# Weight panels of two attentions' neighbours, moved into the attentions in pieces

## The reference, cut to what matters

```python
# first block: differential attention of six heads with two maps each, and attention to a memory
kv = rms_norm(mem, mem_norm_g) @ w_mem_kv          # once for block a, once for block b
proj = h @ w_in                                    # q, k, v, q_mem
a = softmax(q0 @ k0 + bias) - lam * softmax(q1 @ k1 + bias);  o = a @ v
om = softmax(q_mem @ k_mem * 64 ** -0.5) @ v_mem
x = x + concat(rms_norm(o), om) @ w_out
# second block, odd layer: 16 heads of 64, S = 256 is one block, so plain causal attention
q, k, v, g = split(x @ w_in_odd)
o = softmax(rope(q) @ rope(k) * 64 ** -0.5, causal) @ v
x = layer_norm(alpha * x + (o * silu(g)) @ w_out_odd)
```

## Time and profile before

| | |
|---|---|
| runs | 3120.51, 3126.64, 3128.22 us, median 3126.64 us |
| profiled execution, first to last instruction (span; the page gives no other time for it) | 3122.5 us |
| PE busy | 3014.5 us, 97% |
| DVE busy | 2007.9 us, 64% |
| ACT busy | 1512.8 us, 48% |
| mean granted TensorE clock | 0.989 |
| bytes moved | 606.10 MB, mean 194 GB/s |

### The profile page before, as it was taken

One profiled execution on the slowest core, in us unless ns is written; L12 is line 12 of the kernel. 1 busy time (PEld: TensorE's weight loads), 2 busy tenths in 40 slices (PEclk: granted clock), 3 DMA queues, 4 the chain that ended last, 5 costly groups with the idle time before them and its releaser, 6 DMA issues. The chain is left out here.

```text
span 3122.5 us, 43115 instructions
## 1 busy us (share of the span) xinstructions
PE 3014.5 (97%) x17959; PEld 2637.2 (84%) x17959; DVE 2007.9 (64%) x2237; ACT 1512.8 (48%) x1692; POOL 24.1 (1%) x41
## 2 busy tenths in 40 slices
PE   7999998899999999999999999999999999999998
PEld 6889897788888899778888888998789798997898
DVE  4547647555455467498898987554555756787755
ACT  4543343334344345477777776443434445432453
POOL 0001000000000000000000000000000000000000
PEclk9999999999999999999999999999999999999999
DMA  5338650065555567599999998541445143345142
GB/s 194 132 124 265 223 185 28 9 242 189 188 189 184 173 211 243 201 361 351 354 363 350 370 349 298 174 145 60 141 167 177 42 162 135 135 152 177 55 169 95
DMA packets 197852, 606.10 MB, mean 194 GB/s; under 512 B 19648, under 2 KB 59401, under 8 KB 154394
## 3 DMA queue, kind: packets, MB, share of 16 engines
q1 hardware_dynamic: 192306, 588.23, 53.0%
q0 software_dynamic: 3872, 12.71, 1.3%
q10 hardware_dynamic: 1480, 2.41, 0.3%
HBM read 602.26 MB, written 1.05 MB: 193 GB/s over the span
## 5 line engine op out<-in xcount | busy, mean ns | idle before, releaser
L2121 DVE TENSOR_TENSOR w_lo<-ring,w_hi 128x2048 fp32r<-128x2048 f32 x336 | 769.7, 2292 | 336.2 <-ACT w_hi L2016 331.0
L2016 ACT ACTIVATE w_hi<-ring 128x2048 fp32r<-128x2048 f32 x336 | 643.1, 1915 | 367.4 <-PE ps L1963 153.4
L358 DVE TENSOR_TENSOR w_lo<-ring,w_hi 128x2048 fp32r<-128x2048 f32 (+2 forms) x209 | 469.4, 2247 | 480.1 <-ACT w_hi L349 479.4
L349 ACT ACTIVATE w_hi<-ring 128x2048 fp32r<-128x2048 f32 (+2 forms) x209 | 392.7, 1881 | 645.1 <-PE ps L470 488.4
L470 PE MATMUL ps<-h_hi,w_hi 128*128 128x256 f32 x1616 | 463.7, 287 | 17.6 <-DVE w_lo L358 10.7
L470 PE MATMUL ps<-h_lo,w_hi 128*128 128x256 f32 x1616 | 459.7, 284 | 0.0
L470 PE MATMUL ps<-h_hi,w_lo 128*128 128x256 f32 x1616 | 459.5, 284 | 0.0
L470 PEld LDWEIGHTS ps<-h_hi,w_hi 128*128 128x128 f32 x1616 | 312.5, 193 | 22.2 <-issue 17.0
L470 PEld LDWEIGHTS ps<-h_lo,w_hi 128*128 128x128 f32 x1616 | 312.6, 193 | 0.3
L470 PEld LDWEIGHTS ps<-h_hi,w_lo 128*128 128x128 f32 x1616 | 312.6, 193 | 0.0
L1926 PE MATMUL ps<-w_hi,h_hi 128*128 128x512 f32 x672 | 266.6, 397 | 1.4 <-DVE w_lo L2121 1.4
(11 more groups left out here) (539 smaller groups left out, 5544.3 us busy)
## 6 DMA issues: line engine op xcount, KB each, us to landing
ring<-in_moe_w_gate_up SPq DMA_DIRECT2D x224, 1024.0 KB, 4.9
ring<-in_moe_w_down SPq DMA_DIRECT2D x112, 1024.0 KB, 4.9
ring<-in_w_in SPq DMA_DIRECT2D x58, 1024.0 KB, 6.9
ring<-in_w_in_even SPq DMA_DIRECT2D x30, 1024.0 KB, 6.9
ring<-in_dense_w_gate_up SPq DMA_DIRECT2D x22, 1024.0 KB, 7.7
ring<-in_w_in_odd SPq DMA_DIRECT2D x16, 1024.0 KB, 6.7
arena<-in_w_ada POOLq DMA_DIRECT2D x24, 512.0 KB, 4.9
ring<-in_b_w_in SPq DMA_DIRECT2D x12, 1024.0 KB, 6.2
```

Source lines behind the costliest of these rows:

```text
L349: k.nc.scalar.activation(self.part(k.w_hi, b, m), src, ACT.Copy).then_inc(k.hi_ready, 1)
L358: k.nc.vector.tensor_tensor(self.part(k.w_lo, b, m), src, self.part(k.w_hi, b, m).bitcast(F32), ALU.subtract).then_inc(k.lo_ready, 1)
L2016: nc.scalar.activation(high(g, h), raw(g, h), ACT.Copy).then_inc(k.hi_ready, 1)
L2121: nc.vector.tensor_tensor(low(g, h), raw(g, h), high(g, h).bitcast(F32), ALU.subtract).then_inc(k.lo_ready, 1)
```

## The change

The panel of block b's memory leaves `mem_kv` and becomes a job of its own that runs within `diff_attention`. The two gate panels leave `in_odd` and become a job within `block_attention`. Such a job is added with `aside=True`: its group stands in a fourth pair of PSUM banks (6 and 7) with its own `group_read`, the attention then has two score banks in place of three, and its filler of 18 transposes is left out.

A class `Aside` places the work: each panel is cut into eight pieces of 12 matmuls (half, output tile, half of the chunks), which PE does after the scores of the iteration that `pieces` names; the rounding of each further half panel (the last is the first half of the next job) comes at the end of ACT's iteration that `rounds` names, and its rest on DVE in two quarters, at the end of the iterations that `rests` names. ACT evicts a panel in the iteration after its last piece, behind that iteration's rounding.

In `block_attention` the first 14 units' outputs are copied ungated by ACT; the first gate panel is evicted plainly and gets its Silu in iteration 16, the second gets it with its eviction in iteration 17; DVE multiplies chunks 0 to 3 in iteration 17 and 4 to 6 in iteration 18. The last two units are gated as before, the first of them after the second panel's eviction. SP loads panels during these attentions. `input_scales` comes whole before the first panel's eviction.

```diff
+    def evict(self, eng, m, which):          # was a local function of stage
     def place(self, r, i, j):
...
-        m.bank, m.before = group % SLOTS, i + group // SLOTS
+        m.bank, m.before = (SLOTS, r.asides + j) if r.aside else (group % SLOTS, i + group // SLOTS)
...
-    def rest_of_weights(self, dve, m, halves=(0, 1)):
+    def rest_of_weights(self, dve, m, halves=(0, 1), quarter=None):
...
+            if quarter is not None:
+                nk = m.r.part_shape(m.j)[0] // 2
+                at = slice(quarter * nk, (quarter + 1) * nk)
+                last = k.nc.vector.tensor_tensor(w_lo[:, at, :], src[:, at, :], w_hi[:, at, :], ALU.subtract)
+                if quarter == 1:
+                    last.then_inc(k.lo_ready, 1)
+                continue
...
-    return {"act": {2: [lambda: squares(0, k.x, junk), lambda: squares(1, k.x, junk)], 3: [roots]},
-            "dve": {2: [first_half], 3: [scales]}}
+    return {"act": {1: [lambda: squares(0, k.x, junk), lambda: squares(1, k.x, junk), roots]},
+            "dve": {1: [first_half, scales]}}
...
+class Aside:
...
+    def products(self, pe, s):
+        for (q, piece), at in zip(self.blocks, self.pieces):
+            if at == s:
+                self.stream.products(pe, self.place(q), only=piece)
+
+    def half(self, j, prepare):
+        if j < 2 * len(self.panels):
+            prepare(self.place(j // 2), (j % 2,))
+        else:
+            self.stream.first_of_next(prepare)
+
+    def round(self, act, s):
+        for j, at in enumerate(self.rounds, 1):
+            if at == s:
+                self.half(j, lambda m, halves: self.stream.round_weights(act, m, halves))
+        for q in range(len(self.panels)):
+            if self.pieces[8 * q + 7] + 1 == s:
+                self.stream.evict(act, self.place(q), "act")
+        if s in self.act:
+            self.act[s](act)
+
+    def rest(self, dve, s):
+        for j, at in enumerate(self.rests, 1):
+            for quarter in range(2):
+                if at[quarter] == s:
+                    self.half(j, lambda m, halves: self.stream.rest_of_weights(dve, m, halves, quarter))
+        if s in self.dve:
+            self.dve[s](dve)
...
-def attention(k, name, groups, work, last_turns=0, scaled=True):
+def attention(k, name, groups, work, last_turns=0, scaled=True, aside=None):
...
-    score_banks = (0, 1, 6)
+    score_banks = (0, 1) if aside else (0, 1, 6)
+    held = len(score_banks)
...
+        if aside:
+            @st.block.sync
+            def _(sp):
+                k.stream.ahead(sp)
...
                 if s < n_units:
-                    if s >= 3:
-                        pe.wait_ge(exp_done, s - 2)
+                    if s >= held:
+                        pe.wait_ge(exp_done, s - held + 1)
...
+                if aside:
+                    aside.products(pe, s)
                 if 2 <= s <= n_units + 1:
-                    if m == 0:
+                    if m == 0 and not aside:
                         turn_identity(k, 18, 7)
...
             def outputs(m):
-                if is_last and groups[g][4] is not None:
+                if is_last and gated(g):
                     dve.wait_ge(values_done, m + 1)
+                    if late and g == late:
+                        aside.all_read(dve)
...
             for s in range(n_units + 4):       # ACT
                 if s >= 4:
-                    if is_last and groups[g][4] is None:
+                    if is_last and not gated(g):
...
+                if aside:
+                    aside.round(act, s)
...
-    s.add(runs)
+    s.add(runs[0:1])
     s.add([run("F", w["a_w_in"], 0, k.h, to_features(v.qk, scale=0.125)),
...
+    s.add(runs[1:2], aside=True)
...
-    attention(k, "diff_attention", groups + memory_groups(k, v.qm, v.km[0], v.vm[0], v.cat), v.work)
+    attention(k, "diff_attention", groups + memory_groups(k, v.qm, v.km[0], v.vm[0], v.cat), v.work,
+              aside=Aside(s, [0, 0, 1, 2, 4, 6, 8, 10], [-1, 4], [(1, 2), (5, 6)]))
...
-           run("T", wo, 2048, k.h, to_tokens(v.v2), count=2),
-           run("F", wo, 3072, k.h, to_features(v.g2, func=ACT.Silu), count=2)])
+           run("T", wo, 2048, k.h, to_tokens(v.v2), count=2)])
+    s.add([run("F", wo, 3072, k.h, lambda nc, banks, p:
+               to_features(v.g2, func=ACT.Silu if p else ACT.Copy)(nc, banks, p), count=2)], aside=True)
...
+    def finish_gates(act):
+        beside.first_read(act)
+        k.nc.scalar.activation(v.g2[:, 0:4, :], v.g2[:, 0:4, :], ACT.Silu).then_inc(first_gates, 1)
+
+    def gate(first, last, ready):
+        def step(dve):
+            dve.wait_ge(k.out_copied, 2 * last)
+            ready(dve)
+            k.nc.vector.tensor_tensor(v.cat2[:, first:last, :], v.cat2[:, first:last, :], v.g2[:, first:last, :],
+                                    ALU.mult)
+        return step
+
+    beside = Aside(s, [0, 0, 1, 2, 4, 5, 6, 7, 9, 10, 11, 12, 13, 14, 15, 16], [-1, 3, 8, 13],
+                   [(1, 2), (4, 5), (9, 10), (14, 15)], late=14, act={16: finish_gates},
+                   dve={17: gate(0, 4, lambda dve: dve.wait_ge(first_gates, 1)),
+                        18: gate(4, 7, lambda dve: beside.all_read(dve))})
-    attention(k, "block_attention", groups, v.work2, last_turns=8)
+    attention(k, "block_attention", groups, v.work2, last_turns=8, aside=beside)
```

More of the change, by code:

```diff
@@ L259, in __init__, with add @@
         self.flat = []
-        self.groups = self.halves = self.pairs = self.elsewhere = 0
+        self.groups = self.halves = self.pairs = self.elsewhere = self.asides = 0
         self.split_last = (0, 0)
         self.at = 0
-    def add(self, runs):
+    def add(self, runs, aside=False):
         self.jobs.append(runs)
@@ L418, in each_with_next, with products @@
                     step()
-    def products(self, pe, m, by_chunk=False):
+    def products(self, pe, m, by_chunk=False, only=None):
         k, nc, r = self.k, self.k.nc, m.r
@@ L431, in products @@
         for h in range(max(r.parts, 1)):
+            if only and h != only[0]:
+                continue
             kind = r.kinds[h]
@@ L441, in products @@
             for o in range(width // P if kind == "F" else r.tiles):
+                if only and o != only[1]:
+                    continue
+                chunks = range(nk) if not only else range(only[2] * nk // 2, (only[2] + 1) * nk // 2)
                 if r.kind == "R":
@@ L456, in products @@
                 closes = ends and not (r.by_rows and h == 0)
-                for c in range(nk):
+                for c in chunks:
                     if by_chunk and h in (0, r.by_rows) and o == 0:
@@ L475, in products @@
                     last = nc.tensor.matmul(out, k.ones_row[0:1, 0:P], row, start=False, stop=True)
-            if h == 0 and r.parts == 2:
+            if h == 0 and r.parts == 2 and (not only or only == (0, 1, 1)):
                 last.then_inc(k.first_half_used, 1)
-        last.then_inc(k.panel_used, 1)
+        if not only or only == (1, 1, 1):
+            last.then_inc(k.panel_used, 1)
+    def evict(self, eng, m, which):
+        k, r = self.k, m.r
+        if r.on == which and m.j % r.acc == r.acc - 1:
+            eng.wait_ge(k.panel_used, m.number + 1)
+            q = m.p if r.acc == 1 else m.j // r.acc
+            r.evict(k.nc, k.ps[:, 2 * m.bank:2 * m.bank + 2, :], q).then_inc(k.group_read[m.bank], 1)
     def stage(self, name, side=None, extra=(), source=(), features=None, norm=False, heads=None,
@@ L1219, with __init__, place, all_read @@
 WHOLE = (0, S)
+class Aside:
+    def __init__(self, stream, pieces, rounds, rests, late=0, act=None, dve=None):
+        self.stream, self.pieces, self.rounds, self.rests = stream, pieces, rounds, rests
+        self.late, self.act, self.dve = late, act or {}, dve or {}
+        self.panels = [(r, p) for r in stream.jobs[stream.at] for p in range(r.count)]
+        self.blocks = [(q, (h, o, half)) for q in range(len(self.panels))
+                       for h in range(2) for o in range(2) for half in range(2)]
+        assert len(pieces) == len(self.blocks) and all(r.parts == 2 for r, _ in self.panels)
+        assert len(rounds) == len(rests) == 2 * len(self.panels)
+    def place(self, q):
+        r, p = self.panels[q]
+        return self.stream.place(r, 0, p)
+    def all_read(self, eng):
+        m = self.place(len(self.panels) - 1)
+        eng.wait_ge(self.stream.k.group_read[m.bank], m.before + 1)
+    def first_read(self, eng):
+        m = self.place(0)
+        eng.wait_ge(self.stream.k.group_read[m.bank], m.before + 1)
+    def products(self, pe, s):
[23 more added lines that the diff above has]
+            self.dve[s](dve)
 def unit(scores, values, scale=1.0, mask=None, causal=False, n=S, factor=None, floor=False):
@@ L1253, in attention, with out_of, gated @@
     diagonals = work[:, 4:6, :].rearrange("p b (t n) -> p b t n", t=TT)
-    score_banks = (0, 1, 6)
+    score_banks = (0, 1) if aside else (0, 1, 6)
```

(9 more changed lines are left out.)

50 lines of the change are left out of this document (29 added, 21 removed).

## The result

The changed kernel takes 3135.11 us (median of 11 runs, 3128.01 to 3138.27) against 3126.80 us for the kernel before (11 runs in the same session, 3120.51 to 3130.85): a ratio of 1.0026, 95% interval 1.0018 to 1.0034. That is 8.3 us more, inside the range given and 8 us above the time given.

What follows compares the result with a forecast made beforehand. PE, busy 97% of the span, was taken as the bound. Front -14.2, differential attention +8.2 and block half +6.5 (in_odd's -23.0 included) gave +0.5 us, carried to the median as 3127.1 us; range 3117 to 3137.

Steps and rivals of the forecast that it cites:

- the rival's 3138: Block attention: ScalarE becomes the bound, roundings in iterations 3 and 13 stop PE 3.7 and 1.7 us each; chance 0.11.
- gaps of the pieces' own: Differential attention: if each of eight pieces paid its own gap, 0.13 to 0.35 us, 1 to 3 us more.
- front: Start of the kernel: memory panel out -11.5 us, PE's wait -1.0, feature matmuls at full clock -1.7; -14.2 in sum.
- head: First to fifth scores of each attention: 11.2 us after the change, +3.9 in the differential and +4.3 in the block attention.
- pairs: Differential attention, four more pieces in alternate units: a pair goes from 4.41 to 5.42 us, +4.1 over four pairs.
- end: Differential attention: the panel's two eviction halves on ScalarE in iteration 11, 0 to 1 us, taken as 0.2.
- middle: Block attention, iterations 4 to 14: ten units with pieces, one without, and a stall, +17.9 us, plus 1.7 for the clock.
- tail: Block attention, last scores to last product: 12.3 us after the change against 6.68 before, +5.6.
- A piece inherits one gap and costs its stream: Attentions on PE: a piece between scores and transposes inherits the transposes' gap and costs 1.44 us net.
- The stall of iteration 8: Block attention: PE waits 3.7 us before piece 8 in iteration 9, as ScalarE's rounding precedes gate panel 0's eviction; clock adds 1.7.
- Gaps that take the pieces in: Rival, attentions: gaps around pieces close, -6 us, and stall with its clock goes, -5.4, giving 3116; chance 0.14 including the extreme.
- ScalarE as the bound: Rival, block attention: ScalarE's copies and roundings set the pace, 3.6 us with a rounding against PE's 3.56, giving 3138; chance 0.11.

Runs made afterwards that it cites:

- the early piece: The changed kernel with its eighth gate piece one iteration earlier, so gate panel 0 is evicted in iteration 7, ahead of the rounding: 3126.73 us, ratio 1.0003 to before.
- the row scales alone: The kernel before with only input_scales moved beside the first memory panel, all panels left in place: 3122.65 us against 3126.64, ratio 0.9989.

## Why the prediction came out as it did

It named no change of 0.3% or more, and the measured 0.26% agrees, though its interval reaches 0.34%. The mechanism was right and the sum was not: +0.5 us forecast, +8.3 measured, near the rival's 3138. That 3135 is inside the range is in part luck: the room up to 3137 was given for gaps of the pieces' own and late rounds, which did not come, and was filled by falls of the clock that had no term in the sum. Its terms, by the first profile of each kernel:

| step | predicted | measured |
|---|---|---|
| front | -14.2 | -14.5 |
| differential attention | +8.2 | +10.1 (head +5.4 for 3.9, pairs +4.1 for 4.1, end +0.6 for 0.2) |
| in_odd | -23.0 | -23.0 |
| block attention | +29.5 | +32.2 (head +5.8 for 4.3, middle +20.5 for 19.6, tail +5.9 for 5.6) |
| unchanged stages | 0 | +6.2; by two profiles of each, 4.1 in three late stages |

- **A piece inherits one gap and costs its stream** was right: 3.60 us for 3.56 predicted, a pair 5.44 for 5.42, and 2.52 with a quarter of the stream.
- **The front** was right in its parts: the wait, the clock on the features, the panel.
- **The stall of iteration 8** was where and what was predicted, 3.35 us for 3.7. The clock behind it cost 2.5 in place of 1.7: 9.25 - 3.60 - 3.35 = 2.3, and 0.2 in the unit behind. Together 5.9 for 5.4, of which the early piece gave back 5.5.
- **The tail** was 12.45 for 12.3, up to the last product; the stage's +5.9 has 0.7 in it from the slow transposes behind. The load at 2451.10 took 1.28 and its Silu began 0.01 behind it. The Trainium skill's "ScalarE: Activation LUTs" (What ACT_TABLE_LOAD costs) adds a drain of about 1.38 to each switch; neither before nor after does the trace agree, and the sum by the row was the right one.
- **The heads** were mis-sized. "Fifth scores 11.2 us after the first" holds at full clock (11.21 and 11.27). In five of seven profiles of kernels with the whole memory panel in the differential attention, and in four of seven with gate panels in the block attention, the clock fell inside the head, and it took 12.7 to 12.8: 1.5 us in each attention, 3.0 together where both fell. I had read from the earlier trace rows that 1.54 us of idle leave the clock at 1.00. That was one execution: with the row scales alone it fell behind the same idle time (0.52, shown above) in a head of the old order, and cost 0.5 there, where PE has waits of its own.
- **The unchanged stages** had no term. That was the larger miss: 4.1 us in in_conv, compressed_keys and sparse_attention, where the clock fell more than before; why it did is not shown.
- **The rivals.** Gaps that take the pieces in: no, units with a piece pay 1.49 us more than without. ScalarE as the bound: no, the rounds of iterations 3 and 13 stopped nothing, only the one in iteration 8.

So the order of the whole was seen: 37.5 us leave mem_kv, in_a and in_odd, and what comes back in the attentions, where PE's queue is full already, is as much or more (37.7 forecast, 42.3 measured). What was missed is the clock, in the two heads and in the late stages, and by a little behind the stall and at the tail's end.

## What to carry to other kernels

Work moved into a stage whose engine is busy already kept its price here (3.60 us for a unit that took 2.11, with a piece of 1.44); only waits gave something back, such as those in the head of an attention, where four pieces of 5.8 us cost 4.3 at full clock. Before pieces of one job go among the work of another, walk each in-order queue for what stands ahead of the instruction that frees a buffer: here one position in a list cost 5.5 us and another 1.7. Measure an edit that goes with the move by itself: the row scales alone gave 2.7 us by their rows and 4.0 by the median, about as much as any version of the whole.

## What the runs showed of the hardware that was not expected

- The same code met a full or a lowered clock from one execution to the next: with the panel in it the head of the differential attention took 11.2 or 12.7 us, latent_attention 29.3, 33.9 or 35.5.
- A lighter load can be slower: with a quarter of the matmuls in each piece the differential attention took 52.09 us against 50.20, at a granted clock of 0.51 from 118.8 to 139.5.
- The clock's falls in three late stages came with some versions of code that ends some 200 us and more ahead of them, 4.1 us in both profiles of the changed kernel, and not with others.
